# Tokens in four phases in place of two, and three matmuls per convolution tile

## The reference

```
u = rms_norm(h, g_mix);  z = u @ w_in                    # 1024 -> 5120: value, gate, pool, gate A, gate B
a = z_val * sigmoid(z_gate)                              # GLU
a = depthwise_conv(a, width 31, centred) + b_dw
y_conv = silu(layer_norm(a)) @ w_conv_out
m = window_mean(z_pool, windows 2, 4, 8, 16 by channel group) - z_pool
y_pool = (m @ w_pool (per group) * pool_scale) @ w_pool_out
h = h + (sigmoid(z_A + b) * y_conv + sigmoid(z_B + b) * y_pool) @ w_o
v = rms_norm(h, g_ffn);  h = h + (silu(v @ w_ffn_gate) * (v @ w_ffn_up)) @ w_ffn_down
out = rms_norm(h, g_final)
```

## Time and profile before

| | |
|---|---|
| median of 3 runs | 990.5 us (lowest 989.18) |
| profiled execution | 991.0 us |
| its span on the slowest core | 989.5 us (all cores 985.5 to 989.5) |
| PE busy | 962.3 us, 97% |
| DVE, ACT, POOL busy | 433.1, 291.7, 154.9 us |
| mean granted clock of PE, core 0 | 0.997 of full speed |

### The profile page before, as it was taken

The page is one execution under the profiler, slowest core; times in us unless marked ns, Lnnn a source line. Parts: engine busy times, 40 slices in busy tenths (PEclk is TensorE's granted clock), DMA queues, the critical chain, the costliest instruction groups (busy, mean ns, idle before and its releaser), DMA issues.

```text
span 989.5 us, 14699 instructions; the slowest of 8 cores (985.5 to 989.5 us)
## 1 busy us (share of the span) xinstructions
PE 962.3 (97%) x5176; PEld 474.0 (48%) x5176; DVE 433.1 (44%) x632; ACT 291.7 (29%) x486; POOL 154.9 (16%) x216
## 2 busy tenths in 40 slices
PE   3999999999899999999999999999999999999996
PEld 2755555554344444444444444444444444444485
DVE  4776689653885323233476212211112211342454
ACT  3853143356952121110544111111111111121121
POOL 3002221124740000001771110110000000000000
PEclk9999999999999999999999999999999999999999
DMA  9705988775773111226965444553222005122222
GB/s 212 233 4 98 217 215 177 231 171 119 132 170 62 22 20 24 32 32 155 356 165 133 74 82 90 101 98 47 34 31 43 12 1 181 75 85 85 85 86 85
DMA packets 41158, 105.81 MB, mean 107 GB/s; under 512 B 5760, under 2 KB 14208, under 8 KB 38400
## 3 DMA queue, kind: packets, MB, share of 16 engines
q0 software_dynamic: 21472, 51.06, 28.7%
q1 hardware_dynamic: 19616, 53.82, 16.3%
HBM read 115.80 MB, written 21.04 MB: 138 GB/s over the span
## 4 chain that ended last, share of the span: by engine, by line
PE 95%; DMA 2%; DVE 1%; POOL 1%; issue 1%; ACT 0%; DVEq 0%; ACTq 0%; POOLq 0%
PE ps L370 92%; PE ps L664 3%; DMA xb<-xp 1%; DMA wslot<-w_pool_out 1%; DVE uT L397 0%; POOL d L384 0%; DVE h2b L397 0%; POOL wslot L199 0%; ACT sqx L381 0%; DVE sqx L384 0%; ACT ps L381 0%; ACT sq L381 0%; DVE h2b L384 0%; DVEq L1033 0%; DVEq L193 0%
## 5 line engine op out<-in xcount | busy, mean ns | idle before, releaser
L370 PE MATMUL ps<-vT,wslot 128*128 128x512 bf16 x1408 | 304.4, 379 | 0.0
L370 PE MATMUL ps<-uT,wslot 128*128 128x416 bf16 (+3 forms) x1536 | 292.3, 349 | 3.1 <-DVE uT L397 2.3
L370 PEld LDWEIGHTS ps<-uT,wslot 128*128 128x128 bf16 x1536 | 151.1, 99 | 140.8 <-issue 12.6
L370 PEld LDWEIGHTS ps<-vT,wslot 128*128 128x128 bf16 x1408 | 137.7, 98 | 167.1 <-issue 1.6
L384 DVE TENSOR_TENSOR fT<-ps,sgf 128x512 bf16<-128x512 f32 x88 | 60.7, 691 | 228.8 <-PE ps L370 228.8
L370 PE MATMUL ps<-fT,wfd 128*128 128x512 bf16 (+1 forms) x880 | 153.2, 336 | 0.0
L381 ACT ACTIVATE sgf<-ps 128x512 f32<-128x512 f32 x88 | 52.5, 597 | 241.5 <-PE ps L370 234.2
L370 PEld LDWEIGHTS ps<-fT,wfd 128*128 128x128 bf16 x880 | 86.1, 98 | 67.8 <-issue 1.7
L370 PE MATMUL ps<-cell,wslot 128*128 128x512 bf16 x512 | 114.8, 379 | 0.0
L397 DVE SCALAR_TENSOR_TENSOR zt<-zt,ps 128x512 f32<-128x512 f32 x64 | 43.9, 687 | 106.1 <-PE ps L370 106.0
L381 ACT ACTIVATE zt<-ps,hb 128x512 f32<-128x512 f32 x64 | 43.9, 691 | 138.1 <-PE ps L370 138.1
(11 more groups left out here) (76 smaller groups left out, 610.6 us busy)
## 6 DMA issues: line engine op xcount, KB each, us to landing
rep<-ad SPq DMA_DIRECT2D x128, 129.5 KB, 4.7
wslot<-w_in POOLq DMA_DIRECT2D x40, 256.0 KB, 7.0
h1d<-h1b SPq DMA_DIRECT2D x4, 2048.0 KB, 10.1
h2b<-h1d SPq DMA_DIRECT2D x4, 2048.0 KB, 13.7
h1b<-xr SPq DMA_DIRECT2D x3, 2048.0 KB, 19.6
out<-h2b SPq DMA_DIRECT2D x3, 2048.0 KB, 8.1
wslot<-w_ffn_gate POOLq DMA_DIRECT2D x22, 256.0 KB, 5.3
wslot<-w_ffn_up POOLq DMA_DIRECT2D x22, 256.0 KB, 5.2
```

The costliest lines, as they stand in the source:

```text
L370: S.op(PE, lambda e: e.matmul(out, lhsT=lhsT, rhs=rhs, start=start, stop=stop), [lhsT, rhs], [out], signal=stop if signal is None else signal)
```

## The change

Tokens are kept in four phases (token index modulo 4) in place of two, through the whole kernel: `uT`, `psb`, `aT`, `mT`, the convolution's rows (8 channels x 4 phases x 4 shifts on the partitions, 32 channels x 4 phases in a PSUM tile), inputs and outputs on the host. A convolution of 31 taps now takes 3 accumulation steps in place of 4. The window sums are formed between phases, on four rows of 256 in place of one of 1024; where a neighbour is in the next group of four, an add is split in two. The two PSUM tiles of a group are now two sets of 32 channels, each with all 2048 tokens in four phases; the LayerNorm halves the sums of the two on DVE ahead of one product each. Means and scale stay in PSUM for both halves.

```diff
-HALO = 15
+HALO = 16
+PH = 4
-HE = EXT // 2
-HP = PW // 2
+HE = EXT // PH
+HP = PW // PH
...
-        act(alt(psb[c][:, o:o + n]), par(b[:, 0:n]), AF.Copy)
+        act(psb[c][:, :, o // PH:(o + n) // PH], par(b[:, 0:n]), AF.Copy)
...
         if wd == 2:
-            out.append(lambda: (tt(DVE, m, alt(src[:, 0:n]), own, ALU.subtract),
+            out.append(lambda: (tt(DVE, m[:, 1:4, :], p[:, 0:3, x0:x0 + n], own[:, 1:4, :], ALU.subtract),
+                                tt(DVE, m[:, 0, :], p[:, 3, x0 - 1:x0 - 1 + n], own[:, 0, :], ALU.subtract),
...
-        while step < wd:
-            nw = width - step
-            dst = (s1, s2)[tgl][:, 0:nw]
-            out.append(lambda dst=dst, a=src[:, 0:nw], b=src[:, step:step + nw]:
-                       tt(DVE, dst, a, b, ALU.add))
...
+        lo = {4: 1, 8: 1, 16: 2}[wd]
+        wa = n + {4: 1, 8: 2, 16: 4}[wd]
+        b0 = x0 - lo
+        out.append(add((s1[:, 0:3, 0:wa], p[:, 0:3, b0:b0 + wa], p[:, 1:4, b0:b0 + wa]),
+                       (s1[:, 3, 0:wa], p[:, 3, b0:b0 + wa], p[:, 0, b0 + 1:b0 + 1 + wa])))
+        if wd == 4:
+            out.append(add((s2[:, 2:4, 0:n], s1[:, 0:2, 1:1 + n], s1[:, 2:4, 1:1 + n]),
+                           (s2[:, 0:2, 0:n], s1[:, 2:4, 0:n], s1[:, 0:2, 1:1 + n])))
+            src = s2[:, :, 0:n]
+        else:
+            wc = wa - 1
+            out.append(add((s2[:, 0:2, 0:wc], s1[:, 0:2, 0:wc], s1[:, 2:4, 0:wc]),
+                           (s2[:, 2:4, 0:wc], s1[:, 2:4, 0:wc], s1[:, 0:2, 1:1 + wc])))
+            out.append(add((s1[:, :, 0:wc - 1], s2[:, :, 0:wc - 1], s2[:, :, 1:wc])))
...
-            for j in range(4):
-                for r in range(2):
-                    src = bass.AP(a_d, (128 * c + 64 * i + 16 * j) * EXT + HE * r, [[EXT, 16], [1, 4], [1, RW]])
-                    S.dma(SP, rep_sem[r_i], rep[r_i][r::2, j, 0:RW], src, val=tot)
+            for j in range(8):
+                src = bass.AP(a_d, (128 * c + 64 * i + 8 * j) * EXT, [[HE, 32], [1, 4], [1, RW]])
+                S.dma(SP, rep_sem[r_i], rep[r_i][:, j, 0:RW], src, val=tot)
...
-            for h in range(2):
+            for i in range(2):
                 ps = nb()
-                for q in range(4):
+                for q, x0 in enumerate((0, 4, 5)):
                     for j in range(4):
...
-                act(d_sb[g][:, h * TT:(h + 1) * TT], ps[:], AF.Identity, bias=bd)
+                bd = pcc(PC_BDW, 2 * g + i)
+                act(dcell[g // 2][:, :, 2 * (g % 2) + i, :], two(ps[:]), AF.Identity, bias=bd)
...
+    def ln_stat():
+        pm, pq = psum[6], psum[7]
+        for acc, ps in ((acc_s, pm), (acc_q, pq)):
+            tt(DVE, acc[:, :, 0, :], acc[:, :, 0, :], acc[:, :, 1, :], ALU.add)
+            mm(two(ps[:]), pmask[:], acc[:, :, 0, :], True, True)
...
     def silu(h, c):
-        for g in (2 * c, 2 * c + 1):
-            act(actX[g][h], dpart(g, h), AF.Silu, bias=pc[:, PC_LNB + g:PC_LNB + g + 1],
-                scale=pc[:, PC_LNG + g:PC_LNG + g + 1])
-        for g in (2 * c, 2 * c + 1):
-            r0 = 64 * (g % 2)
-            S.dma(SP, rg_sem[h * KC + c], cell[c][r0:r0 + 64, :, h, 1, :], actX[g][h], val=32)
+        for q in range(4):
+            G = 4 * c + q
+            act(cell[c][:, h, q, 0, :], dcell[c][:, h, q, :], AF.Silu, bias=pcc(PC_LNB, G), scale=pcc(PC_LNG, G))
+        for q in range(4):
+            S.dma(SP, rg_sem[h * KC + c], cell[c][32 * q:32 * q + 32, h, :, 1, :], cell[c][:, h, q, 0, :], val=64)
...
-            mm(b[:], lhsT, rhs(k), k == 0, k == KC - 1)
+            mm(two(b[:]), lhsT, rhs(k), k == 0, k == KC - 1)
...
-        x0 = (HALO + b % 2) // 2 + (b // 2) * TT
-        return lambda k: uT[:, k, 1 - b % 2, x0:x0 + TT]
+        x0 = HALO // PH + 256 * (b // 2)
+        return lambda k: uT[:, k, 2 * (b % 2):2 * (b % 2) + 2, x0:x0 + 256]
...
+    cw = np.zeros((NG, 8, PH, 4, 2, 3, 4, 8, PH), f32)
+    for q in range(3):
+        for a in range(4):
+            if q == 2 and a < 3:
+                continue
+            for pi in range(PH):
+                for po in range(PH):
+                    tap = PH * (4 * q + a if q < 2 else 8) + pi - 1 - po
```

More of the change, by code:

```diff
@@ L41 @@
 NX = len(PIECES)
-RW = TOK // 2 + 12
-RWP = 1040
-HALVES = ((0, 1024), (1024, 1024))
+RW = TT + 5
 S_W = 1040
@@ L294, in build_nc @@
     z = oZ
[L295 to L298, removed]
+    RB = 16 * HE
+    rep = [at(f"rep{i}", [128, 8, HE], BF16, o) for i, o in
+           enumerate((z, z + RB, oB + 6 * EXT * 4, oB + 7 * EXT * 4, z + 24064, z + 32384))]
+    z += 2 * RB
+    dsq = [at("dsq0", [128, 2, 2, 256], F32, z), at("dsq1", [128, 2, 2, 256], F32, oW + 8192)]
     z += 4096
@@ L301, in build_nc @@
     z += 2 * PW * 4
-    aT = [at(f"aT{i}", [128, 2, HE], BF16, z + i * EXT * 2) for i in range(2)]
+    aT = [at(f"aT{i}", [128, PH, HE], BF16, z + i * EXT * 2) for i in range(2)]
     z += 2 * EXT * 2
-    s1 = at("s1", [128, S_W], F32, z)
-    s2 = at("s2", [128, S_W], F32, z + S_W * 4)
+    s1 = at("s1", [128, PH, S_W // PH], F32, z)
+    s2 = at("s2", [128, PH, S_W // PH], F32, z + S_W * 4)
     z += 2 * S_W * 4
+    cw.append(at("cw3", [128, 2, 3, 4, 32], BF16, z))
+    z += 1536
+    pmask = at("pmask_s", [128, 128], F32, z)
+    z += 512
     assert z <= oZ + NZT * 2048, (z - oZ, NZT * 2048)
@@ L522, in add_squares @@
         a_, b_, w_ = ((0, 2, 2), (4, 6, 2), (0, 4, 2), (0, 1, 1))[i]
-        dst = sqx[:, a_:a_ + w_, o:o + n]
-        tt(DVE, dst, dst, sqx[:, b_:b_ + w_, o:o + n], ALU.add)
+        dst = sq(a_, w_, p)
+        tt(DVE, dst, dst, sq(b_, w_, p), ALU.add)
     def s1_stat(p):
@@ L528, in s1_stat @@
         st = psum[6][:, 0:n]
-        mm(st, ones[:], sqx[:, 0, o:o + n], True, True)
+        mm(par(st), ones[:], sqx[:, 0, :, o // PH:(o + n) // PH], True, True)
         act(st, st, AF.Ln, bias=e_rms)
@@ L553, in windows, with add @@
         out = []
[L554 to L560, removed]
+        n = 256
+        x0 = HALO // PH + n * ti
+        p = psb[c]
+        m = mT[:, c, :, n * ti:n * ti + n]
+        own = p[:, :, x0:x0 + n]
+        def add(*parts):
+            return lambda: [tt(DVE, o, a, b_, ALU.add) for o, a, b_ in parts]
@@ L573, in windows @@
-        assert width == n
+        lo = {4: 1, 8: 1, 16: 2}[wd]
[12 more added lines that the diff above has]
+            out.append(add((s1[:, :, 0:wc - 1], s2[:, :, 0:wc - 1], s2[:, :, 1:wc])))
+            src = s1[:, :, 0:n]
+            if wd == 16:
+                out.append(add((s2[:, :, 0:n], s1[:, :, 0:n], s1[:, :, 2:2 + n])))
+                src = s2[:, :, 0:n]
@@ L612, in load_cw @@
     def load_cw(g):
-        S.dma(POOL, cw_sem[g % 4], cw[g % 4][:].rearrange("p j q m -> p (j q m)"), cw_d.ap()[g])
+        S.dma(POOL, cw_sem[g % 4], cw[g % 4][:].rearrange("p i q j m -> p (i q j m)"), cw_d.ap()[g])
     def vg(c):
@@ L733, in C @@
         stt(DVE, zt[i][:], zt[i][:], 1.0, ps[:], ALU.add, ALU.mult)
-        tt(DVE, mrg[c][b], zt[i][:], zt[j][:], ALU.add)
+        tt(DVE, mrg[c][b], two(zt[i][:]), two(zt[j][:]), ALU.add)
         zfree.append(i)
@@ L838, in build_nc @@
     Bm(0, 2)
-    for h in range(2):
-        ln_stat(h)
+    ln_stat()
     Bm(0, 3)
     release("gB0")
-    for h in range(2):
-        ln_rstd(h)
+    ln_rstd()
     bg.extend(ln_steps(0))
@@ L944, in build_nc @@
             for k in range(KC):
-                mm(ps[:], w(f"wo{c}", k), mrg[k][b], k == 0, k == KC - 1)
+                mm(two(ps[:]), w(f"wo{c}", k), mrg[k][b], k == 0, k == KC - 1)
             h = h1b[b][:, c, :]
@@ L1135, in _gather @@
 def _gather(results, core):
-    o = np.asarray(results[core]["out"]).reshape(2, 2, 128, KC, TT)
-    return o.transpose(0, 4, 1, 3, 2).reshape(TOK, D)
+    o = np.asarray(results[core]["out"]).reshape(2, 2, 128, KC, 2, 256)
+    return o.transpose(0, 5, 1, 4, 3, 2).reshape(TOK, D)
 _NC_CACHE = {}
```

163 lines of the change are left out of this document (76 added, 87 removed).

## The result

The changed kernel takes **1055.1 us** in the median (1049.7 to 1060.3) against 990.4 us before: ratio 1.0637, 95% interval 1.0617 to 1.0656. The forecast was 986.5 us.

The account below looks back on a forecast made before the run. PE bounds the kernel, busy 962.3 of 989.5 us, so only shortening its list or making it wait counts. Quads -7.1, VectorE +2.1, gathers +1.2, LayerNorm -1.2, fold +0.6 make -4.4 us: 986.5 us, range 985 to 989.

Parts of the forecast that it names:

- Costed at nothing too: PE addresses, start-up squares and norms, and ScalarE's start-up copies: no cost, columns equal or copies hidden by VectorE's norms.
- I add nothing: Store of the GLU output, cut into runs of 624 and 416 B: no added time; second store lands after 3.1 us.
- rival 4: SP's price follows the rows, 1.19 us a transfer; last convolution's gather 28 us late, about 1011 us; chance 0.04.
- SP's price: Issuing a convolution gather transfer on SP: does not follow the number of rows, kept at 16 x 0.69 us a tile.
- the sum: All terms over the whole kernel: -7.1 + 2.1 + 1.2 - 1.2 + 0.6 = -4.4 us.
- Quads, 0.89 us a tile: Convolution matmuls on PE: 12 quads a channel tile, 2.68 us in place of 3.57, 7.1 us gained over eight tiles.
- VectorE between convolutions, 2.1 us: Value/gate tiles after convolutions 1 and 2: PE waits 1.0 and 1.25 us for VectorE's product; 2.1 us lost, ends 1.1 and 2.9.
- Gathers, 1.2 us at the last convolution: Last convolution: wait of 0.6 us for its gather, plus 0.6 for more packets and weights; ends 0 and 4.3.
- Slack is short only at the last tile: Convolution gathers: only the last tile's arrives near its need, at 21.2 against 22.8 us before the change.
- rival 2: Short stores of the GLU output land late, every gather starts 3.1 us later, 989.5 us; chance 0.13.
- LayerNorm statistics, -1.2: LayerNorm after the last convolution: four fp32 passes fewer give 1.7 us, PE waits 0.5; gain 1.2, ends 0.5 and 1.7.
- the fold, +0.6: Folding of weights: SiLU in four activations makes ScalarE's last copies late; loss of 0.6 to 1.7 us, 0.6 taken.

Follow-up runs that it names:

- e3: The changed kernel with 16-byte scheduler granules, but accesses of uT alone rounded out to 32 bytes again; ratio 1.0300 to the kernel before.
- e1: The changed kernel with the scheduler's bookkeeping granule at 16 bytes in place of 32; ratio 1.0071 to the kernel before.
- e10: e5 with only the even channel groups gathered, odd groups reading the group before; ratio 0.9956 to the kernel before, 985.8 us median.
- e5: e4 with the pooling sums also run two at a time in the first two value/gate tiles; 998.6 us in one comparable execution, no ratio.
- e4: e1 with the first four groups of convolution weights loaded ahead of the first value/gate tile; ratio 1.0094 to the kernel before.
- e8: e4 with the pooling weights that POOL asks for at 181 to 214 us held back to about 228; ratio 1.0106 to the kernel before.

## Why the prediction was wrong

**The step that failed** is the last of the parts: "Costed at nothing too: addresses in two or four runs on PE, start-up squares and norms (equal columns)", and with it "I add nothing" for the store. Both price what an instruction does and leave out which waits the new layout puts in front of it. The start-up norms have equal columns, and 25.1 us went in front of the first value/gate tile (table), 25.7 with `uT` alone in e3. The store's landing, 4.6 us for the larger part before and 6.1 after, was of no interest while only the gather waited for it; behind the false wait it stood in VectorE's way seven times, 44.4 us. I took the scheduler at its word, a wait wherever bytes are shared, and did not ask in what unit it counts and whether the new row lengths divide by it. 2080 and 1248 B divide by 32; 1040 and 624 B don't. None of the rivals contained it either; rival 4, the one far on the slower side, was wrong too: SP's price is 590 ns.

**Without those waits the terms of the sum can be read off**, since e1 is the change without them, and e10 is that with half of the gathers and e5's two moves. e10's core mean is 4.5 us below that of before (982.9 against 987.4), the sum said 4.4; that is luck, since e10 has no gather wait (1.2 in the sum), waits less on VectorE, and loses more behind the fold. By terms:

- *Quads, 0.89 us a tile*: right within 0.1. From one convolution to the next is 16.9 us in e1 where nothing waits, 17.7 before; convolutions 5 and 6, which follow one another, start 2.6 us apart against 3.5.
- *VectorE between convolutions, 2.1 us*: right in place and mechanism, waits of 0.97 and 1.04 us in the row (1.0 and 1.25 forecast); from convolution 1 to 2 and from 2 to 3 it is 18.0 and 18.1 us in place of 16.9. VectorE's timeline in e1 has the sums 2.86 us and the end of the first product 13.5 us after convolution 1 began at 145.8, where the earlier trace rows gave 13.49. A split pair takes 1.30 us where one instruction took 1.23, hence the 0.07:

```profile
148.66 1.23 DVE L389 TENSOR_TENSOR acc_s<-acc_s,d 128x1024 f32<-128x1024 f32 x1 [0.85 <-ACT d L386]
...
157.52 1.30 DVE L389 TENSOR_TENSOR s<-s 128x514 f32<-128x514 f32 x2
158.74 0.59 DVE L389 TENSOR_TENSOR aT<-ps,sg 128x416 bf16<-128x416 f32 x1
```

- *Gathers, 1.2 us at the last convolution*: too small, and too narrow a place. "Slack is short only at the last tile" was a wrong reading: on core 0 of before the gathers of tiles 6 and 0 land 2.4 and 3.6 us before their convolutions begin (215.1 and 217.5, 121.4 and 125.0), those of tiles 1 to 5 6.6 us or more, and convolutions 6 and 0 are where the waits came. SP's price was right in the median (603 ns in e1) but not in the mean, 776 ns against 626, since three times as many issues take over 0.9 us; and the engines' share was not carried from 0.84 through every stage. Beyond the 2.79 us of an undisturbed one, convolutions 0, 6 and 7 take 1.8 to 5.5 us a core in e1's profile, 3.6 on average; over all runs, where the slowest core counts, e1 and e10 are 1.15% or 11.4 us apart. Twice the packets take more of the engines: by the trace's packet times 47 ns for 1034 B against 85 ns for 2072 B in the median, 62.6 us of 16 engines for the gathers against 55.6, and 21.4 against 16.3 for the convolution's weights.
- *Stores*: rival 2 had the mechanism of a late store by half. In e1 the second one lands after 4.9 us, the first after 6.1, against 3.1 and 4.6. The Trainium skill (DMA: Bandwidth & Descriptors, Specifications) counts transfers below 512 B as read, modified and written; stores with runs of 416 B landed later by a factor of 1.3 (after) to 1.6 (e1), those with runs of 624 B, above that bound, by 1.3, so no step at 512 B can be told from these two.
- *LayerNorm statistics, -1.2, and the fold, +0.6*: the stage from convolution 7 to the first pooling product became 1.7 us shorter in e1 (30.1 against 31.8; -0.9 for the quads and -1.2 make -2.1). PE waits 0.84 us for `acc_s` (0.5 forecast). The fold was mis-sized: the wait for the last folded weights is 2.26 us on core 5 in e10 (1.01 on that core before), and the stage in which it lies is 1.7 us longer in the core means (0.6 forecast, 1.7 the far end):

```profile
262.75 2.77 PE L375 MATMUL ps<-mT,weff 128*128 128x512 bf16 x6 [2.26 <-ACT weff L386]
```

**The miss of 68.6 us in two parts.** By its ratio e1 stands at 1.0071 x 990.4 = 997.4 us: 57.7 us of the miss are the false waits together with the low clock of the slowest pair of cores, 10.9 are in e1. The second part is the gathers: with half of them e10 takes 985.8 us, 0.7 below the forecast, and e5, from which it differs by them alone, 998.6. It alone would have put the time above the range, whose far end for the gathers was 4.3.

## What to carry to other kernels

When a change alters row lengths or offsets, divide the new ones by the unit in which dependencies are tracked, before anything is priced: rows that end inside a unit make neighbours wait for each other, and instruction counts and durations do not show it. When a wait goes away and the time stays, look at the next shared resource's share in that same stage; here the gathers, with the transfer engines at 0.94, took what PE gave. Of a stage that is full on two resources, a saving on one is worth only the slack of the other: ask by how much each transfer lands ahead of its reader, and at which tiles.

## What the runs showed of the chip

A wait is paid twice. In e4, core 5, PE stood still in convolution 6's wait; the granted clock fell to 0.50, the 1.2 GHz level, and was still there for the matmuls that followed (window, length, busy by engine, PEclk, DMA share, GB/s):

```profile
210.00:215.00 5.00, 4.21 (x73) 1.72 (x72) 2.69 (x3) 4.11 (x8) 2.91 (x5) 1.00 0.77 189
215.00:220.00 5.00, 0.00 (x0) 0.00 (x0) 4.90 (x5) 2.94 (x6) 0.00 (x0) 0.74 0.92 135
220.00:225.00 5.00, 0.00 (x0) 0.00 (x0) 0.00 (x0) 0.00 (x0) 0.00 (x0) 0.50 1.02 190
225.00:230.00 5.00, 4.70 (x29) 1.62 (x30) 0.98 (x1) 2.54 (x4) 0.00 (x0) 0.50 0.98 299
```

In the changed kernel the stretch with the seven waits stands at 0.84 on core 1, its convolution matmuls average 443 ns (380 to 396 on the cores of e1), and its PE is busy longer with less to do. That is not the price of the waits alone: core 4, with seven such waits of its own, stands at 0.94 in the same window (438 ns), and core 0 stays at 0.81 in a stretch where its PE is never idle. What holds cores 0 and 1 there stays open (core 4, then core 0):

```profile
156.00:292.00 136.00, 118.97 (x829) 57.73 (x827) 83.23 (x107) 55.52 (x95) 31.17 (x43) 0.94 0.72 161
```

```profile
280.00:300.00 20.00, 20.00 (x113) 8.14 (x112) 5.28 (x5) 9.97 (x17) 7.53 (x7) 0.81 0.66 147
```

A gather does not come equally late on all cores. In e4 and e8, at engine shares of 0.8 to 1.0, some cores had the gather for convolution 6 landed 2.4 to 5.8 us after its last issue and others 8.1 to 12.4 us after: cores 4 and 5 were late in e4, 3, 6 and 7 in e8. What picks them stays open.
